# Copies of branch C's caches issued in the delta rule instead of in branch B's prompt part

## The reference

```python
xn = rmsnorm(x, norm_mix);  h = xn @ w_in                  # model width 1024
# A: RWKV-7 with 6 heads of 64: per token, state S (64 x 64 per head)
S = S * w_t + (S @ -kk_t) (kk_t * a_t)^T + v_t k_t^T;  out = S @ r_t
# B: stick-breaking attention, 4 heads; the samples also attend to 4096 past tokens in pages
# C: dilated window attention, 3 groups (window 128, 512, 2048; dilation 1, 4, 16), 2 heads each
ext = concatenate([buf, stack([k[:, :, hs], v[:, :, hs]], axis=2)], axis=1)
new_bufs.append(ext[:, -min(win, ext.shape[1]):])          # the new cache of the group
x = x + (sum of gated branches) @ w_out;  x = x + ConvFFN(rmsnorm(x, norm_ffn))
```

## Time and profile before

| | us |
|---|---|
| median of 3 runs | 2694.86 |
| lowest and highest run | 2694.41, 2695.11 |
| the profiled execution's own time | 2698.43 |
| its span, first to last instruction | 2696.4 |
| PE busy | 2301.4 (85%) |
| PEld busy | 2090.5 (78%) |
| DVE busy | 1226.7 (45%) |
| ACT busy | 421.7 (16%) |
| POOL busy | 656.0 (24%) |

### The profile page before, as it was taken

One profiled execution on the slowest core, in us unless ns is written; L12 is line 12 of the kernel. 1 busy time (PEld: TensorE's weight loads), 2 busy tenths in 40 slices (PEclk: granted clock), 3 DMA queues, 4 the chain that ended last, 5 costly groups with the idle time before them and its releaser, 6 DMA issues. The chain is left out here.

```text
span 2696.4 us, 45967 instructions
## 1 busy us (share of the span) xinstructions
PE 2301.4 (85%) x19363; PEld 2090.5 (78%) x19363; DVE 1226.7 (45%) x1835; ACT 421.7 (16%) x639; POOL 656.0 (24%) x598
## 2 busy tenths in 40 slices
PE   3995699769766776995599999798999999999995
PEld 3994688649434446974499999798999999999985
DVE  2336443221876671177123223118753762772652
ACT  4004212110751220032000001002100000110012
POOL 3110100001554331100012212143432432432331
PEclk6996899879888898997699999899999999999997
DMA  5140100041929985132511111211111111111112
GB/s 153 47 164 3 27 4 4 18 156 30 319 82 349 331 274 172 31 142 108 170 41 41 49 39 31 98 47 32 48 36 51 46 36 51 41 42 45 48 39 73
DMA packets 255424, 237.24 MB, mean 88 GB/s; under 512 B 22060, under 2 KB 243094, under 8 KB 253549
## 3 DMA queue, kind: packets, MB, share of 16 engines
q1 hardware_dynamic: 208096, 160.08, 19.3%
q10 hardware_dynamic: 39452, 53.37, 5.9%
q0 software_dynamic: 7680, 20.98, 2.3%
HBM read 211.10 MB, written 45.11 MB: 95 GB/s over the span
## 5 line engine op out<-in xcount | busy, mean ns | idle before, releaser
L134 PE MATMUL ps<-ml,fu_wh 128*128 128x352 f32 (+1 forms) x1248 | 410.4, 329 | 22.0 <-POOL fu_wl L128 16.9
L136 PE MATMUL ps<-mh,fu_wl 128*128 128x352 f32 (+1 forms) x1248 | 409.2, 328 | 0.0
L135 PE MATMUL ps<-mh,fu_wh 128*128 128x352 f32 (+1 forms) x1248 | 409.0, 328 | 0.0
L134 PEld LDWEIGHTS ps<-ml,fu_wh 128*128 128x128 f32 x1248 | 235.9, 189 | 23.9 <-POOL fu_wl L128 23.1
L128 POOL TENSOR_TENSOR fu_wl<-fu_wt,fu_wh 128x1024 fp32r<-128x1024 f32 (+2 forms) x84 | 191.4, 2279 | 246.0 <-DVE fu_wh L123 246.0
L135 PEld LDWEIGHTS ps<-mh,fu_wh 128*128 128x128 f32 x1248 | 236.7, 190 | 0.0
L136 PEld LDWEIGHTS ps<-mh,fu_wl 128*128 128x128 f32 x1248 | 235.5, 189 | 0.0
L134 PE MATMUL ps<-mx_l,wgh 128*128 128x352 f32 (+1 forms) x576 | 195.8, 340 | 22.3 <-POOL wgl L128 11.3
L136 PE MATMUL ps<-mx_h,wgl 128*128 128x352 f32 (+1 forms) x576 | 190.2, 330 | 0.0
L135 PE MATMUL ps<-mx_h,wgh 128*128 128x352 f32 (+1 forms) x576 | 190.1, 330 | 0.0
L134 PE MATMUL ps<-fu_al,fu_wh 128*128 128x384 f32 x528 | 176.6, 334 | 10.7 <-POOL fu_wl L128 7.1
(11 more groups left out here) (474 smaller groups left out, 4727.6 us busy)
## 6 DMA issues: line engine op xcount, KB each, us to landing
fu_wt<-in_w_up SPq DMA_DIRECT2D x44, 512.0 KB, 3.8
out_win_sample<-in_cache_win SPq DMA_DIRECT2D x8, 2040.0 KB, 38.1
bs_pk<-in_cache_sb_k SPq DMA_DIRECT2D x112, 128.0 KB, 7.7
bs_pv<-in_cache_sb_v SPq DMA_DIRECT2D x112, 128.0 KB, 7.7
wgt<-in_w_in SPq DMA_DIRECT2D x24, 512.0 KB, 4.1
bs_pk<-in_cache_sb_k POOLq DMA_DIRECT2D x80, 128.0 KB, 5.7
bs_pv<-in_cache_sb_v POOLq DMA_DIRECT2D x80, 128.0 KB, 5.9
fu_wt<-in_w_down SPq DMA_DIRECT2D x24, 384.0 KB, 3.2
```

Source lines behind the costliest of these rows:

```text
L134: nc.tensor.matmul(out, wh, xl, start=start, stop=False)
L135: nc.tensor.matmul(out, wh, xh, start=False, stop=False)
L136: return nc.tensor.matmul(out, wl, xh, start=False, stop=stop)
```

## The change

The 24 copies are issued by the same engine with the same addresses in the delta rule, right behind the loads of the sample states and ahead of the wait for the prompt state. They count on a new semaphore, `win`, and SyncE waits for it at the end of the delta rule's list. In branch B's prompt part the copies are gone, and the last wait on `st` is for the four stores of k and v alone.

```diff
     x = {n: g.sem(f"dx_{n}") for n in ("c", "sr", "am", "zi", "wi", "tr", "s0", "tp", "tk", "pr", "cp", "z", "ze", "pl", "lv",
-                                       "y", "ye", "u", "ue", "vx", "ux", "o", "oe", "sn", "se", "ft", "fa", "fv", "out")}
+                                       "y", "ye", "u", "ue", "vx", "ux", "o", "oe", "sn", "se", "ft", "fa", "fv", "out", "win")}
@@ delta, SyncE
             for b in range(NB):
                 eng.dma_start(sr[:, b], a["state_wkv"][0, b].rearrange("h v k -> v h k")).then_inc(x["sr"], 16)
+            for gi in range(3):
+                W = P * DILS[gi]
+                for b in range(NB):
+                    eng.dma_start(g.o[f"win{gi}_sample"][0, b, 0:W - NQ].rearrange("t a h d -> t (a h d)"),
+                                  a[f"cache_win{gi}"][0, b, NQ:W].rearrange("t a h d -> t (a h d)")).then_inc(x["win"], 16)
             eng.wait_ge(s["fe"], 1)
...
             eng.wait_ge(x["out"], 16 * NB)
+            eng.wait_ge(x["win"], 16 * 3 * NB)
@@ b_prompt, SyncE
                 eng.dma_start(later[:, :], a["c_later"]).then_inc(s["c"], 16)
-                for gi in range(3):
-                    W = P * DILS[gi]
-                    for b in range(NB):
-                        eng.dma_start(g.o[f"win{gi}_sample"][0, b, 0:W - NQ].rearrange("t a h d -> t (a h d)"),
-                                      a[f"cache_win{gi}"][0, b, NQ:W].rearrange("t a h d -> t (a h d)")).then_inc(s["st"], 16)
                 eng.wait_ge(s["ka"], NT // 2 + 1)
...
-                eng.wait_ge(s["st"], 64 + 16 * 3 * NB)
+                eng.wait_ge(s["st"], 64)
```

## The result

The changed kernel takes 2727.73 us (2725.70 to 2728.81, 4 runs) against 2694.99 us (2694.41 to 2698.82, 4 runs): ratio 1.0119, 95% interval 1.0103 to 1.0135. By the medians it is 32.7 us slower, outside the range of the forecast and at the price of its first rival (2727).

What follows compares the result with a forecast made beforehand. It took compute to bound the prompt part (DVE full) and PE the delta rule. Removed 0 and added 0 on the median of 2694.86 gave 2695 us, range 2687 to 2720.

Steps and rivals of the forecast that it cites:

- first rival: PE in the delta rule, 296 to 369 us: late code fetches starve it, up to 32 us, 2727 us; chance 0.27.
- What bounds the kernel: Branch B's prompt part is set by compute, with DVE full; the delta rule is bound by PE.
- what is removed: Prompt part: 24 issues, 16.32 us of SP, go; SP only idles longer at the block's end, worth 0.
- SP and the data queues: Delta rule: copies issued from 295.8 us land by 369, 128 us before the prompt state's store; sum 0.
- Where the change touches TensorE: Delta rule: 17 or 18 of PE's 16 KB code packets must get past the copies; taken as 0.
- most turns find a packet half done: Delta rule: a code packet takes about 1.6 + 1.13 = 2.7 us, well below 4.17, so 0.
- The rule of turns: DMA engines go round between queues a whole packet at a time; price 0 to 1.9 us in the delta rule.
- How far ahead the code comes: PE's fetches in the delta rule have slack of a size that the trace doesn't show; 0 taken.
- Rival 1: Code fetches starve PE in the delta rule once one takes over 4.17 us: 32 us, 2727 us; chance 0.27.
- the evidence against: PE didn't wait for code in the prompt part under the same copies, though it used few; one packet's turn just fits.

Runs made afterwards that it cites:

- e3: The changed kernel with the 24 copies and their wait left out: 2698.01 us against 2698.04 for the kernel before, ratio 1.0005.
- e7: The changed kernel with the copies issued as 104 transfers of at most 255 KB, unpaced: 2711.21 us, ratio 1.0065 to the kernel before.
- e6: The changed kernel with SyncE waiting for each copy to land before issuing the next: 2715.87 us, ratio 1.0093 to the kernel before.
- e4: The changed kernel with each copy spread over 8 DMA engines instead of 16: 2709.83 us, ratio 1.0055 to the kernel before.

## Why the prediction was wrong

- *What bounds the kernel, what is removed, SP and the data queues*: right. SP issued the copies in 17.09 us, they landed by 312.5 + 57.2 = 369.7 us at the latest (forecast 369), far ahead of the store of the prompt state, and the prompt part gained nothing (e3). SP waited 111.6 us at its end (about 100 said).
- *Where the change touches TensorE*: the place was right, code packets against copies in 296 to 369 us; the value was wrong. The step that failed is "most turns find a packet half done (about 1.6 + 1.13 = 2.7 us ...)", so "I take 0". A code packet doesn't wait for the rest of one copy packet: under the 2040 KB copies it started 6.5 to 7.6 us after PE had entered the block before, instead of about 0 to 1.2, and PE ran its code another 2.2 to 2.4 us later, where the prediction counted 1.13 us. That makes some 9.4 us a block against 4.17, and 33.67 us in the stage against 0. The wait falls only from 7.2 to 4.3 us when the pieces get thirty times smaller, and to between 0.2 and 2.8 us when two or four transfers are in flight: it is the backlog already given to the DMA engine that counts.
- *The rule of turns* (the Trainium skill, "DMA: Bandwidth & Descriptors", section "Queues, rings and completion order", a whole packet of typically 9 to 17 descriptors each turn): the prediction took the page's packet for one row of the profile, a single 65 KB piece, and priced 0 to 1.9 us. Read as a batch it points the right way, but no run here follows its numbers. By an estimate from the page's figure and 20.7 GB/s for one DMA engine, 17 pieces of 2.2 KB are 1.8 us of work, and 9 of 65 KB are 28; the next code packet started 4.3 and 7.2 us after PE's entry.
- *How far ahead the code comes*: I left this open ("of a size that the trace doesn't show") and then used the kind answer. Of the two figures that the Trainium skill gives in "Runtime: NRT & Kernel Launch", section "Instruction fetch mechanics", 128 KiB would be eight blocks and 29 us in hand at 4.17 each; the traces side with the two blocks of the same section. The trace before held the answer, once one knows where its blocks begin: each packet started 2.9 to 4.8 us before PE entered its block, of which 2.3 are needed, so only 0.6 to 2.5 us were to spare. And the fetches were not mostly hidden.
- *Rival 1* named engine, place and turning point (a block each 4.17 us), and 2727. That its number fits to 1 us is in part luck: it had 9.8 blocks 3.26 us late each, and the run has seven stops, with blocks 8.9 to 9.9 us apart under the 2040 KB copies. It deserved more than 0.27: the fetches' slack was unknown, the price of one turn already touched the limit, and the evidence against (no stall in the prompt part) came from a stage that fetches a block each 30 us.

Open: what caps the wait. Between PE's entry and the next code packet a DMA engine could copy some 150 KB at 65 KB pieces (7.2 us at the 20.7 GB/s of 65.3 KB in 3.15 us) and some 90 KB at 2 KB pieces (4.3 us), although far more is queued in both; with eight 16 KB pieces in flight it is 3.9 us, and with no limit on them (e7) 5.1. And what the 2.3 us between a packet's start and PE's entry consist of isn't shown, beyond the packet's own 1.1 us of transfer.

## What to carry to other kernels

Code is a transfer too: before bulk copies are put beside a stage, see how far apart the packets of the instruction queue come there (one each 4 us has no room for a wait, one each 30 us has plenty), since the stretch with the emptiest DMA queues can be the one most sensitive to them. If copies must lie there, cap what is in flight: with transfers of at most 255 KB, two in flight cost at most 0.17% and four at most 0.34%, an open queue of them 0.65%, and the whole copies 1.2%. And a slack that no row shows is to be priced from the rival's side, or measured: count 256 instructions to a block, and see how long before PE's entry its packet starts.

## What the runs showed of the hardware that I had not expected

Code packets of 16 KB, 1.1 us of transfer each, come 7 us apart behind a full queue even of 2 KB pieces, and the packet's own transfer time in the rows doesn't change (0.7% of 16 x 20 us for two, 1.1 us each): the delay is nowhere in the busy figures, only in the distance of the packets. PE's code came one block ahead, with 0.6 to 2.5 us to spare where a block lasts 4.17 us. One 2040 KB copy in flight is enough to use that up (e6). And half of the DMA engines left free saves only about half of the loss (e4).
